# The first projection in eight units of 256 tokens, its LayerNorm on two engines and its weight casts on three, and two value products moved between the key and query products

## The chip, the cores and the metric

The kernel runs on one core of a Trainium2 chip. The metric is the device time in microseconds (us) of the whole program. Five engines work side by side and each runs its own list of instructions strictly in order, waiting on semaphores: TensorE (PE, matmuls and transposes), VectorE (DVE), ScalarE (ACT), GpSimd (POOL) and SyncE (SP, which here only issues DMA transfers). SBUF is the on-chip memory, PSUM the accumulators that TensorE writes.

## The reference, cut to what matters

One layer over 16 learned meta tokens and 512 tokens of width 1024: a first LayerNorm, one wide projection whose columns are the queries, keys and values of a sparse branch (A), its indexer, the low-rank latents of a dense branch (B) and two gates; then attention in both branches, 8 heads each, and an output projection with a second LayerNorm.

```
h = layer_norm(concat([meta, x]), ln_emb_g, ln_emb_b)
qa, ka, va, ga, qi, ki, wi, cq, ckv, kpe, gb = split(h @ w_in)
qb = rms_norm(cq) @ w_uq;  k_nope, vb = rms_norm(ckv) @ w_ukv;  rotary on q_pe and k_pe
A: scores of the indexer -> top 128 keys of each query -> softmax over them with a relative bias -> oa
B: causal softmax over all keys -> ob
out = layer_norm(ALPHA * h + concat([oa * silu(ga), ob * silu(gb)]) @ w_out, ln_post_g, ln_post_b)
```

## The kernel before, in words

**Layout.** The normalised input is held transposed, features on the partitions: `hh` and `hl`, 8 chunks of 128 features by 528 tokens. A float32 value is carried as a high part (rounded to the matmul's type, `hh`) and a low part (what the rounding left, `hl`); weights likewise as `wh` and `wl`. Each product is three matmuls: high by high, high by low, low by high. Weights come in blocks of 128 columns (`BLOCKS`), by DMA into one of three `raw` buffers, are cast to `wh` by ACT (`high_part`, L576) and subtracted into `wl` by POOL (`low_part`, L569).

**One list for all engines.** `schedule()` writes one list, `ORDER`, of stages: ("W", b) prepares weight block b, ("J", kind, n, m) is one product of the projections (a "job"), ("S", g) the scores of head g, ("X", g) its exponentials, ("R", g) its division, ("TP", g) and the job "tq" its transposes, ("PV", pair, part) the product with the values, ("TOPK", round, half) one round of the search for the top keys. Every engine walks the same list and takes its own part of each stage, in this order. Heads g = 0 to 7 are the dense branch, two heads to a pair, and 8 to 15 the sparse one. During the dense heads, DVE also does the 14 rounds of the search (MAX8 and MATCH_REPLACE8), between its other work.

**The first job.** Ahead of the list stands the opening. DVE takes the statistics of the meta tile and the four token tiles (L961, L962, L969), ACT the square root and the normalisation in place (L755, L760). TensorE passes the time with dummy transposes (`busy`, L1280). When all five tiles are normalised, it transposes chunk by chunk (`spread(c)`, L1302, four 128x128 transposes into the PSUM bank `hbank(c)`); DVE and ACT in turns apply gain and bias on the bank (L994, L767), ACT rounds it to `hh` (L772), DVE subtracts to `hl` (L999). TensorE multiplies each chunk by the first two weight blocks, which make the latent query "cq": two matmuls of 512 columns each at L1382, L1387 and L1391, and the last chunk at L1399. DVE casts these two weight blocks (L989), POOL makes their low parts in two instructions (L664), and the next product is "ckv" (L1319).

**Places the change touches later.** "qn" and "kn" are the dense branch's per-pair queries and keys: q of pair p+1 is put between the scores and the exponentials of head g = 2p+1, its two k products after the division. They are emptied from PSUM by ACT and DVE, one half each (L823, L1066; L827, L1070). "va" are the value rows of the sparse branch, four row blocks of 128 and a short one, twice; ACT alone empties them (L836). A job writes one of two PSUM banks in turn and waits until that bank's previous job has been emptied; the scores of the next pair wait until its q and both k are emptied.

Of the kernel before, what the change touches and what calls it, by code (L numbers as in the profile page):

```python
# [25 lines left out]
P = 128  # L26
# [70 lines left out]
HIGH_BY_DVE = [b in (("cq", 0), ("cq", 1)) for b in BLOCKS]  # L97
# [17 lines left out]
def schedule():  # L115
# [84 lines left out]
    for g in range(2 * HEADS):  # L200
# [124 lines left out]
def build(nc, x, meta, ln_emb_g, ln_emb_b, rel_bias, ln_post_g, ln_post_b, weights, gains, onehot, cos_t,  # L325
# [6 lines left out]
    with ctx:  # L332
# [107 lines left out]
        w_high_dve = sem("w_high_dve")  # L440
        scaled = sem("scaled")
# [103 lines left out]
        def low_made(eng, b):  # L545

            eng.wait_ge(w_low, max(LOW_BY_DVE[:b + 1].count(False), 2))
# [10 lines left out]
        def high_made(eng, b):  # L558

            if HIGH_BY_DVE[b]:  # L560
                eng.wait_ge(w_high_dve, HIGH_BY_DVE[:b + 1].count(True))
            else:
                eng.wait_ge(w_high, HIGH_BY_DVE[:b + 1].count(False))

# [39 lines left out]
        def _(sp):  # L604
            sp.dma_start(x_meta, meta).then_inc(x_in[4], 16)
            for t in range(QT):
# [31 lines left out]
        def _(pool):  # L638
# [15 lines left out]
            for i in range(QT):  # L654
                last = mask[:, POFF[i] + NK[i] - 144:POFF[i] + NK[i]]
                pool.affine_select(out=last, in_=last, compare_op=ALU.is_ge, fill=MASKED, base=META,
                                   pattern=[[-1, 144]], channel_multiplier=1).then_inc(made, 1)
            for stage, *arg in ORDER:
                if stage == "W":
                    if arg[0] == 0:  # L660
                        pool.wait_ge(w_high_dve, 2)
                        for n in range(0, DC, DC // 2):
                            c = slice(n, n + DC // 2)
                            pool.tensor_tensor(wl[:, c, 0:2 * P].rearrange("p c (b n) -> p b c n", b=2), raw[:, 0:2, c, :],  # L664
                                               wh[:, c, 0:2 * P].rearrange("p c (b n) -> p b c n", b=2).bitcast(F32),
                                               ALU.subtract).then_inc(w_low, 1)
# [989 lines left out]
```

## Time and profile before

| | us |
|---|---|
| median of 3 runs | 334.42 |
| lowest, highest run | 333.64, 335.16 |
| the profiled execution, its own time | 335.0 |
| its span, first to last instruction | 333.2 |

The profiled execution is 0.6 us slower than the median, and 1.8 us of its time lie outside the span. Its mean granted TensorE clock is 0.991 of full speed. "Busy" is the time in which an engine has an instruction running; in a timeline, the bracket at the end of a row is how long the engine sat idle before it, and what it was released by. Matmuls overlap, so a row's duration is longer than the step from one start to the next.

### The profile page before, as it was taken

To read this page: it belongs to the slowest core of one execution; us is meant where nothing else is said; L and a number is where in the kernel's file an instruction comes from. 1 tells how busy PE (TensorE), PEld (TensorE's weight loads), DVE (VectorE), ACT (ScalarE), POOL (GpSimd) and SP (SyncE) were. 2 spreads that over 40 slices of the span, in tenths; PEclk is the share of its full clock that TensorE was granted. 3 is DMA by queue.
4 is the path that set the end of the run, shared out by engine and by line. 5 is a ranking of instruction groups with operands and counts; after the bars stand their busy time and mean duration, and the time that the engine had idled before them with its cause. 6 is when DMAs were issued, how large, how long until landed. Compare 5 with 4: busy or idle time off the path is not lost.

```text
span 333.2 us, 6144 instructions
## 1 busy us (share of the span) xinstructions
PE 319.4 (96%) x2098; PEld 275.9 (83%) x2098; DVE 235.9 (71%) x626; ACT 174.6 (52%) x382; POOL 199.2 (60%) x240
## 2 busy tenths in 40 slices
PE   8799999999999999989999999999999999999990
PEld 7588987778787888878797988897978898998990
DVE  5784720259965699999995995478787866564686
ACT  4685754343543355467545664677587753722220
POOL 6260899988432251556633589699859582660552
PEclk9799999999999999999999999999999999999998
DMA  7455432428513033202400232222323110130033
GB/s 270 190 147 223 131 94 95 128 74 296 176 63 127 1 107 100 79 0 73 136 2 16 65 129 97 91 77 92 98 92 95 66 35 30 66 126 2 2 122 130
DMA packets 11710, 32.86 MB, mean 99 GB/s; under 512 B 2409, under 2 KB 2793, under 8 KB 11681
## 3 DMA queue, kind: packets, MB, share of 16 engines
q1 hardware_dynamic: 8944, 26.89, 23.7%
q10 hardware_dynamic: 2736, 5.59, 5.5%
q8 instruction: 17, 0.28, 0.3%
q14 instruction: 13, 0.10, 0.1%
HBM read 29.83 MB, written 4.81 MB: 104 GB/s over the span
## 4 chain that ended last, share of the span: by engine, by line
PE 82%; DVE 10%; issue 2%; DMA 2%; ACT 2%; SPq 1%; DVEq 0%
PE ps_j L1319 50%; PE ps_o L1579 6%; PE ps_s L1530 4%; PE ps_s L1534 3%; DVE iw L1146 3%; PE ps_t L1319 3%; PE ps_s L1503 2%; DVE top L1142 2%; PE ps_t L1549 2%; DMA iw<-in_onehot 2%; PE ps_j L1371 2%; PE ps_t L1554 2%; ACT pr L910 1%; PE ps_j L1419 1%; PE ps_j L1382 1%
## 5 line engine op out<-in xcount | busy, mean ns | idle before, releaser
L569 POOL TENSOR_TENSOR wl<-raw,wh 128x1024 fp32r<-128x1024 f32 (+2 forms) x33 | 78.1, 2374 | 56.9 <-ACT wh L576 56.8
L1319 PE MATMUL ps_j<-hh,wh 128*128 128x512 f32 (+2 forms) x216 | 75.2, 348 | 0.1
L1319 PE MATMUL ps_j<-hl,wh 128*128 128x512 f32 (+2 forms) x216 | 74.7, 346 | 0.0
L1319 PE MATMUL ps_j<-hh,wl 128*128 128x512 f32 (+2 forms) x216 | 74.4, 345 | 0.0
L705 POOL TENSOR_SCALAR pr<-pr,rden 128x528 f32<-128x528 f32 (+1 forms) x64 | 35.3, 572 | 42.5 <-DVE rden L1186 42.5
L1319 PEld LDWEIGHTS ps_j<-hh,wh 128*128 128x128 f32 (+1 forms) x216 | 40.3, 186 | 6.3 <-issue 0.5
L1319 PEld LDWEIGHTS ps_j<-hh,wl 128*128 128x128 f32 (+1 forms) x216 | 40.3, 187 | 5.1
L1319 PEld LDWEIGHTS ps_j<-hl,wh 128*128 128x128 f32 (+1 forms) x216 | 40.3, 186 | 5.1
L910 ACT ACTIVATE pr<-pr,mn 128x528 f32<-128x528 f32 (+1 forms) x64 | 36.0, 564 | 14.4 <-DVE mn L1175 14.3
L576 ACT ACTIVATE wh<-raw 128x1024 fp32r<-128x1024 f32 (+2 forms) x35 | 35.9, 1040 | 0.4 <-DMA raw<-in_weights 0.4
L723 POOL TENSOR_TENSOR bm<-bias,mask 128x144 f32<-128x144 f32 (+3 forms) x32 | 27.5, 895 | 0.0
L1146 DVE MATCH_REPLACE8 iw<-top,iw 128x512 f32<-128x512 f32 (+2 forms) x42 | 22.6, 542 | 0.0
L1142 DVE MAX8 top<-iw 128x8 f32<-128x512 f32 (+2 forms) x42 | 21.8, 547 | 0.1
L814 ACT ACTIVATE mix<-ps_j 128x512 f32<-128x512 f32 x7 | 4.2, 599 | 30.2 <-PE ps_j L1319 30.2
L1530 PE MATMUL ps_s<-k_b,q_b 96*128 96x240 f32 (+4 forms) x80 | 19.5, 390 | 0.0
L1076 DVE TENSOR_TENSOR ks<-ps_j,ks 64x264 fp32r<-64x264 f32 x32 | 13.8, 430 | 7.0 <-ACT ks L848 6.2
L1319 PE MATMUL ps_j<-wh,mbh 128*128 128x256 f32 x64 | 18.4, 287 | 0.0
L1319 PE MATMUL ps_j<-wl,mbh 128*128 128x256 f32 x64 | 18.1, 283 | 0.0
L1319 PE MATMUL ps_j<-wh,mbl 128*128 128x256 f32 x64 | 18.1, 283 | 0.0
L848 ACT ACTIVATE ks<-ps_j 64x264 fp32r<-64x264 f32 x32 | 12.3, 386 | 9.3 <-PE ps_j L1319 8.6
L1319 PE MATMUL ps_j<-wh,hh 128*128 128x256 f32 x56 | 17.0, 304 | 0.0
L920 ACT ACTIVATE pt<-ps_t 128x512 f32<-128x512 f32 x16 | 9.6, 598 | 13.6 <-PE ps_t L1549 7.7
(292 smaller groups left out, 832.8 us busy)
## 6 DMA issues: line engine op xcount, KB each, us to landing
raw<-in_weights SPq DMA_DIRECT2D x37, 512.0 KB, 3.3
bias_by_distance<-bias_vector ACTq DMA_DIRECT2D x1, 2624.0 KB, 12.7
bias<-bias_by_distance ACTq DMA_DIRECT2D x8, 264.0 KB, 2.9
res<-in_x SPq DMA_DIRECT2D x4, 512.0 KB, 5.2
out<-res SPq DMA_DIRECT2D x3, 512.0 KB, 2.6
pt<-in_ln_emb_g SPq DMA_DIRECT2D x1, 512.0 KB, 5.5
pt<-in_ln_emb_b SPq DMA_DIRECT2D x1, 512.0 KB, 6.5
q_b<-qpe ACTq DMA_DIRECT2D x8, 64.0 KB, 2.0
```

The lines of the kernel that those rows point to most:

```text
L569: eng.tensor_tensor(ring_of(False, b), raw_of(b), ring_of(True, b).bitcast(F32), ALU.subtract).then_inc(done, 1)
L576: act.activation(ring_of(True, b), raw_of(b), ACT.Copy).then_inc(w_high, 1)
L705: pool.tensor_scalar(a, a, rden[:, k, n:n + 1], 1.0, ALU.mult, ALU.mult).then_inc(scaled, 1)
L723: pool.tensor_tensor(bm[:, h % 2, s], bias[:, h % 4, T - NK[i]:T], mask[:, s], ALU.add).then_inc(folded, 1)
L848: act.activation(ks[HD * v:HD * v + HD, e, v, 264 * m:264 * m + 264], bank[HD * e:HD * e + HD, 0:264], ACT.Copy).then_inc(job_act, 1)
L910: act.activation(dst, dst, ACT.Exp, bias=mn[:, k, n:n + 1], scale=-1.0, accum_out=den[:, k, n:n + 1]).then_inc(e_done, 1)
L1076: dve.tensor_tensor(ks[HD - HD * v:P - HD * v, e, v, s], bank[HD * e:HD * e + HD, 0:264], ks[HD * v:HD * v + HD, e, v, s].bitcast(F32), AL ...
L1142: dve.max(top8[:, i, :], a).then_inc(done, 1)
L1146: dve.match_replace(out=a, in_to_replace=top8[:, i, :], in_values=a, imm_value=TAKEN).then_inc(done, 1)
L1319: last = pe.matmul(dst, a, b, start=n == 0 and part[0], stop=n == count - 1 and part[1])
L1530: last = pe.matmul(dst, q_b[:, e, i * P:(i + 1) * P], k_b[:, e, a:b], start=True, stop=True)
L1579: last = pe.matmul(ps_o[HD * e:HD * e + HD, q0:NQ], v[:, j, c:c + HD], pt[:, e, CO[j]:CO[j] + NQ - q0], start=j == 0, stop=j == 4)
```

## The change

**Opening.** The first job is cut into 8 units: unit u is two feature chunks (2i, 2i+1, with i = u mod 4) by 256 tokens (the first half for u < 4). The first half needs only token tiles 0 and 1, so TensorE can begin with those. Normalisation: ACT does the meta tile and tile 0 as before; tiles 1, 2 and 3 are done by DVE, each in two `tensor_scalar` instructions of 512 columns on SBUF. Gain and bias are two instructions of 256 columns each per unit, on DVE for units 1, 5, 7 and on ACT for the others. The first two weight blocks arrive in halves between the token tiles; the first halves are cast by ACT and DVE, the second halves and the whole of block 2 by POOL, which also makes the low parts in four steps in place of two. The six dummy transposes ahead of each of two waits go, and the first 36 become 30. The four DVE instructions on the meta columns now come after the last unit's low part. The last unit's low products are ordered by bank: two matmuls finish the first cq product, two the second; before, six finished each.

**List.** At g = 1 (pair 0) the job va(0, 2) moves from behind the division to a place ahead of qn(1), between the scores and the exponentials. At g = 5 (pair 2) the job va(1, 2) moves from ahead of kn(3, 0) to between kn(3, 0) and kn(3, 1).

The diff, cut to what matters (shifted counts of semaphores, and the statistics that are only rewritten as functions, are left out):

```diff
-HIGH_BY_DVE = [b in (("cq", 0), ("cq", 1)) for b in BLOCKS]
+FIRST_BLOCKS = 2
+GAIN_BY_DVE = [u in (1, 5, 7) for u in range(DC)]
...
-            if g % 2 and more:
-                jobs = [("qn", p + 1)] + jobs + [("kn", p + 1, 0), ("kn", p + 1, 1)]
+            if g == 1:
+                jobs += [("qn", p + 1), ("kn", p + 1, 0), ("kn", p + 1, 1)]
+            elif g % 2 and more:
+                jobs = [("qn", p + 1), ("kn", p + 1, 0)] + jobs + [("kn", p + 1, 1)]
...
-        if jobs[0][0] == "qn":
-            order.append(("QPE", jobs[0][1]))
-            job(*jobs.pop(0), extra=0)
+        if ("qn", p + 1) in jobs:
+            order.append(("QPE", p + 1))
+            while jobs[0][0] != "kn":
+                job(*jobs.pop(0), extra=0)
...
+        def unit(u):
+            i, a = u % 4, u // 4
+            return (2 * i, 2 * i + 1), slice(META + 256 * a, META + 256 * a + 256)
...
+            tile_in(0)
+            tile_in(1)
             sp.dma_start(gain[:, :], gains).then_inc(par_in, 16)
             sp.dma_start(rb[:, :], rel_bias).then_inc(par_in, 16)
             sp.dma_start(oh_sb, onehot).then_inc(oh_in, 16)
-            for b in range(len(BLOCKS)):
+            tile_in(2)
+            for half in range(2):
+                c = slice(4 * half, 4 * half + 4)
+                for b in range(FIRST_BLOCKS):
+                    sp.dma_start(raw[:, b, c, :], weights[b, :, c, :]).then_inc(raw_in[b] if half else first_in[b], 16)
+                if half == 0:
+                    tile_in(3)
...
+            def first_low(n):
+                c = slice(2 * n, 2 * n + 2)
+                pool.tensor_tensor(wl[:, c, 0:2 * P].rearrange("p c (b n) -> p b c n", b=2), raw[:, 0:2, c, :],
+                                   wh[:, c, 0:2 * P].rearrange("p c (b n) -> p b c n", b=2).bitcast(F32),
+                                   ALU.subtract).then_inc(w_low, 1)
+            pool.wait_ge(w_first_act, 1)
+            pool.wait_ge(w_high_dve, 1)
+            first_low(0)
+            first_low(1)
+            for b in range(FIRST_BLOCKS):
+                pool.wait_ge(raw_in[b], 16)
+                pool.tensor_copy(wh[:, 4:8, b * P:b * P + P], raw[:, b, 4:8, :]).then_inc(w_high_pool, 1)
+            pool.wait_ge(w_high_pool, 2)
+            first_low(2)
+            first_low(3)
+            pool.wait_ge(raw_in[2], 16)
+            pool.tensor_copy(ring_of(True, 2), raw_of(2)).then_inc(w_high_pool, 1)
...
+            def gains_of(u):
+                act.wait_ge(x_t, u + 2)
+                for n, c in enumerate(unit(u)[0]):
+                    half = hbank(u)[:, 256 * n:256 * n + 256]
+                    act.activation(half, half, ACT.Identity, bias=bcol[:, c:c + 1],
+                                   scale=gcol[:, c:c + 1]).then_inc(h_aff_act, 1)
+            def high(u):
+                chunks, s = unit(u)
...
+                act.activation(hh[:, chunks[0]:chunks[1] + 1, s], hbank(u).rearrange("p (c n) -> p c n", c=2),
+                               ACT.Copy).then_inc(h_high, 1)
+            deviation(0)
+            normal(0, 2)
+            deviation(1)
+            normal(1, 4)
+            deviation(2)
...
+            act.activation(wh[:, 0:4, 0:P], raw[:, 0, 0:4, :], ACT.Copy).then_inc(w_first_act, 1)
             act.wait_ge(par_in, 32)
...
+            gains_of(0)
+            high(0)
+            high(1)
+            deviation(3)
+            gains_of(2)
+            high(2)
+            gains_of(3)
+            deviation(4)
+            high(3)
+            gains_of(4)
+            high(4)
+            high(5)
+            gains_of(6)
+            high(6)
+            high(7)
...
+            def inverse(n, done):
+                t, r = TILES[n]
+                dve.wait_ge(root, n + 1)
+                dve.reciprocal(rstd[0:r, t:t + 1], rstd[0:r, t:t + 1]).then_inc(shift, 1)
+                dve.wait_ge(shift, done)
+                if n < 2:
+                    dve.scalar_tensor_tensor(out=nmr[0:r, t:t + 1], in0=mv[0:r, t, 0:1], scalar=-1.0,
+                                             in1=rstd[0:r, t:t + 1], op0=ALU.mult, op1=ALU.mult).then_inc(shift, 1)
+                else:
+                    for x in (0, 512):
+                        part = res[:, t, x:x + 512]
+                        dve.tensor_scalar(part, part, mv[:, t, 0:1], rstd[:, t:t + 1], ALU.subtract,
+                                          ALU.mult).then_inc(xn_dve, 1)
...
+            def low(u):
+                chunks, s = unit(u)
+                dve.wait_ge(h_high, u + 1)
+                c = slice(chunks[0], chunks[1] + 1)
+                dve.tensor_tensor(hl[:, c, s], hbank(u).rearrange("p (c n) -> p c n", c=2), hh[:, c, s].bitcast(F32),
+                                  ALU.subtract).then_inc(h_low, 1)
+            stat(0, 0)
+            stat(0, 1)
+            stat(1, 0)
+            inverse(0, 1)
+            stat(1, 1)
+            stat(2, 0)
+            inverse(1, 3)
+            stat(2, 1)
+            stat(3, 0)
+            inverse(2, 5)
+            dve.wait_ge(first_in[1], 16)
+            dve.tensor_copy(wh[:, 0:4, P:2 * P], raw[:, 1, 0:4, :]).then_inc(w_high_dve, 1)
+            dve.wait_ge(par_in, 32)
+            gains_of(1)
+            stat(3, 1)
+            low(0)
+            low(1)
+            stat(4, 0)
+            stat(4, 1)
+            inverse(3, 6)
+            low(2)
+            inverse(4, 7)
+            low(3)
+            gains_of(5)
+            low(4)
+            gains_of(7)
+            low(5)
+            low(6)
+            low(7)
...
-            busy(36)
-            pe.wait_ge(xn_done, 1)
...
+            def high(u):
+                chunks, s = unit(u)
+                a = 256 * (u // 4)
+                if u % 4 < 2:
+                    pe.wait_ge(w_first_act, 1)
+                    pe.wait_ge(w_high_dve, 1)
+                else:
+                    pe.wait_ge(w_high_pool, 2)
+                pe.wait_ge(h_high, u + 1)
+                for c in chunks:
+                    for k in range(2):
+                        pe.matmul(ps_j[:, k, a:a + 256], wh[:, c, k * P:k * P + P], hh[:, c, s], start=c == 0, stop=False,
+                                  skip_group_check=True)
+                pe.wait_ge(w_low, u % 4 + 1)
+                for c in chunks:
+                    for k in range(2):
+                        pe.matmul(ps_j[:, k, a:a + 256], wl[:, c, k * P:k * P + P], hh[:, c, s], start=False, stop=False,
+                                  skip_group_check=True)
+            def low(u):
+                chunks, s = unit(u)
+                a = 256 * (u // 4)
+                pe.wait_ge(h_low, u + 1)
+                for k in range(2):
+                    for c in chunks:
+                        last = pe.matmul(ps_j[:, k, a:a + 256], wh[:, c, k * P:k * P + P], hl[:, c, s], start=False,
+                                         stop=c == DC - 1, skip_group_check=True)
+                    if u == DC - 1:
+                        last.then_inc(job_mm, 1)
...
+            pe.wait_ge(xn_act, 2)
+            pe.wait_ge(xn_dve, 1)
+            spread(0)
+            spread(1)
+            pe.wait_ge(xn_dve, 2)
+            spread(2)
+            spread(3)
+            high(0)
+            high(1)
+            low(0)
+            low(1)
+            high(2)
+            high(3)
+            low(2)
+            pe.wait_ge(xn_dve, 6)
+            spread(4)
+            spread(5)
+            low(3)
+            spread(6)
+            high(4)
+            spread(7)
+            low(4)
+            high(5)
+            low(5)
+            high(6)
+            low(6)
+            high(7)
+            low(7)
```

**How instructions stand.** On DVE in the opening, before (the end of the statistics, then the meta columns, the weight casts and the chunks):

```order
L966 RECIPROCAL rstd<-rstd 128x1
L972 SCALAR_TENSOR_TENSOR nmr<-mv,rstd 128x1
L979 TENSOR_TENSOR iw<-ps_t,gain 128x128
L981 TENSOR_TENSOR iw<-iw,gain 128x128
L983 CAST hh<-iw 128x8x16
L985 TENSOR_TENSOR hl<-iw,hh 128x8x16
L989 CAST wh<-raw 128x8x128 x2
L994 TENSOR_SCALAR ps_s<-ps_s,gain 128x512
L999 TENSOR_TENSOR hl<-ps_s,hh 128x512
L994 TENSOR_SCALAR ps_t<-ps_t,gain 128x512
L999 TENSOR_TENSOR hl<-ps_o,hh 128x512
L999 TENSOR_TENSOR hl<-ps_t,hh 128x512
```

On DVE now, from the second half of tile 2's statistics to unit 3's low part (`res<-res,mv,rstd` is the normalisation of a token tile):

```order
L1032 BN_STATS st<-res 128x6
L1035 BN_AGGR mv<-st 128x2
L1065 TENSOR_TENSOR hl<-ps_s,hh 128x2x256
L1065 TENSOR_TENSOR hl<-ps_o,hh 128x2x256
L1032 BN_STATS st<-res 128x6 x2
L1035 BN_AGGR mv<-st 128x2
L1041 RECIPROCAL rstd<-rstd 128x1
L1049 TENSOR_SCALAR res<-res,mv,rstd 128x512 x2
L1065 TENSOR_TENSOR hl<-ps_t,hh 128x2x256
L1041 RECIPROCAL rstd<-rstd 128x1
L1049 TENSOR_SCALAR res<-res,mv,rstd 128x512 x2
L1065 TENSOR_TENSOR hl<-ps_s,hh 128x2x256
```

What moved: two token tiles are normalised between the low parts of units 1 and 3, and the meta columns are gone from here. On POOL at the same place before (ahead of the first `wl` row it makes masks), the low parts of blocks 0 and 1, then of 2 and 3:

```order
L652 AFFINE_SELECT ci<-ci 128x128
L656 AFFINE_SELECT mask<-mask 128x144 x4
L664 TENSOR_TENSOR wl<-raw,wh 128x2x4x128 x2
L569 TENSOR_TENSOR wl<-raw,wh 128x8x128
L569 TENSOR_TENSOR wl<-raw,wh 128x8x104
```

and now:

```order
L681 AFFINE_SELECT mask<-mask 128x144 x4
L687 TENSOR_TENSOR wl<-raw,wh 128x2x2x128 x2
L697 CAST wh<-raw 128x4x128 x2
L687 TENSOR_TENSOR wl<-raw,wh 128x2x2x128 x2
L702 CAST wh<-raw 128x8x128
L583 TENSOR_TENSOR wl<-raw,wh 128x8x128
L583 TENSOR_TENSOR wl<-raw,wh 128x8x104
```

What moved: three casts have come to POOL between the low parts. On ACT around the exponentials of head 1, before (`v_a` is va, `q_b` and `k_b` are qn and kn, L910 the exponentials):

```order
L836 ACTIVATE v_a<-ps_j 128x256
L857 DMA q_b<-qpe 32x512 x2
L823 ACTIVATE q_b<-ps_j 64x512
L910 ACTIVATE pr,den<-pr,mn 128x528
L910 ACTIVATE pr,den<-pr,mn 128x272
L910 ACTIVATE pr,den<-pr,mn 128x144
L910 ACTIVATE pr,den<-pr,mn 128x400
L836 ACTIVATE v_a<-ps_j 128x256
L827 ACTIVATE k_b<-ps_j 64x264 x2
L920 ACTIVATE pt<-ps_t 128x512
```

and now:

```order
L905 ACTIVATE v_a<-ps_j 128x256
L926 DMA q_b<-qpe 32x512 x2
L905 ACTIVATE v_a<-ps_j 128x256
L892 ACTIVATE q_b<-ps_j 64x512
L980 ACTIVATE pr,den<-pr,mn 128x528
L980 ACTIVATE pr,den<-pr,mn 128x272
L980 ACTIVATE pr,den<-pr,mn 128x144
L980 ACTIVATE pr,den<-pr,mn 128x400
L896 ACTIVATE k_b<-ps_j 64x264 x2
L990 ACTIVATE pt<-ps_t 128x512
```

What moved: the emptying of va(0, 2) stands ahead of that of qn(1), and so ahead of the exponentials; TensorE's matmuls stand likewise.

In pair 2 one of the two `k_b` copies of ACT goes ahead of the `v_a` one in the same way.

## Rows read from the trace of the kernel before

**Rows 1.** The page's first part: busy time, share of the span, instructions.

```profile
PE 319.4 (96%) x2098; PEld 275.9 (83%) x2098; DVE 235.9 (71%) x626; ACT 174.6 (52%) x382; POOL 199.2 (60%) x240
```

**Rows 2.** Timeline, TensorE, opening: start, duration (us), engine, line, operation, idle before.

```profile
10.64 1.02 PE L1296 MATMUL ps_s<-iw,rb 32*8 32x512 f32 x2 [2.19 <-DMA iw<-in_onehot]
...
14.14 1.11 PE L1302 MATMUL ps_s<-ident,res 128*128 128x128 f32 x4
...
18.42 0.60 PE L1302 MATMUL ps_s<-ident,res 128*128 128x128 f32 x4
...
30.18 0.36 PE L1319 MATMUL ps_j<-hh,wh 128*128 128x264 f32 x1
```

**Rows 3.** Windows by stretch: busy per engine (instructions), granted TensorE clock, DMA share, GB/s.

```profile
13.00:14.00 1.00, 1.00 (x6) 0.93 (x5) 0.97 (x4) 1.00 (x1) 0.00 (x0) 0.50 0.03 12
```

**Rows 4.** Timelines, TensorE, ACT and DVE, around the exponentials of head 1.

```profile
144.46 0.37 PE L1319 MATMUL ps_j<-ckh,wh 128*128 128x264 f32 x1 [0.92 <-ACT v_a L836]
...
141.60 0.74 ACT L910 ACTIVATE pr<-pr,mn 128x528 f32<-128x528 f32 x1 [0.79 <-DVE mn L1175]
...
143.85 0.36 ACT L836 ACTIVATE v_a<-ps_j 128x256 f32<-128x256 f32 x1
...
142.09 0.69 DVE L1066 TENSOR_SCALAR q_b<-ps_j 64x512 f32<-64x512 f32 x1
```

**Rows 5.** Timeline, TensorE, kn(3, 1) of pair 2.

```profile
181.77 0.36 PE L1319 MATMUL ps_j<-ckh,wh 128*128 128x264 f32 x1 [0.31 <-ACT v_a L836]
```

**Rows 6.** Timeline, ACT, opening: meta normalised, gain and bias, rounding, emptying of cq.

```profile
6.47 1.23 ACT L760 ACTIVATE pt<-pt,nmr,rstd 16x1024 f32<-16x1024 f32 x1
...
16.71 0.75 ACT L767 ACTIVATE ps_o<-ps_o,gain 128x512 f32<-128x512 f32 x1
17.48 0.60 ACT L772 ACTIVATE hh<-ps_o 128x512 fp32r<-128x512 f32 x1
...
29.44 0.60 ACT L786 ACTIVATE v_b<-ps_j 128x512 f32<-128x512 f32 x1 [3.49 <-PE ps_j L1399]
```

**Rows 7.** Timeline, DVE, opening: weight casts, gain and bias on PSUM.

```profile
13.26 1.29 DVE L989 CAST wh<-raw 128x1024 fp32r<-128x1024 f32 x2
15.30 0.82 DVE L994 TENSOR_SCALAR ps_s<-ps_s,gain 128x512 f32<-128x512 f32 x1 [0.75 <-PE ps_s L1302]
```

**Rows 8.** Groups by form, POOL: busy us, mean ns, idle before.

```profile
L569 POOL TENSOR_TENSOR wl<-raw,wh 128x512 fp32r<-128x512 f32 x1 | 1.3, 1302 | 0.1
...
L690 POOL COPY k_b<-k_b 32x528 f32<-32x528 f32 x1 | 0.6, 622 | 0.1
```

**Rows 9.** Timelines, POOL and DVE, 75 to 81 us: both on SBUF.

```profile
75.86 2.39 POOL L569 TENSOR_TENSOR wl<-raw,wh 128x1024 fp32r<-128x1024 f32 x1 [0.80 <-ACT wh L576]
78.33 1.66 POOL L685 TENSOR_TENSOR k_b<-k_b,cos_sb 32x528 f32<-32x528 f32 x1
...
75.96 2.84 DVE L1102 SCALAR_TENSOR_TENSOR v_b<-v_b,gain,pr 128x512 f32<-128x512 f32 x1
...
75.96 4.57 DVE L1102 SCALAR_TENSOR_TENSOR v_b<-v_b,gain,pr 128x512 f32<-128x512 f32 x2
```

**Rows 10.** Timelines, DVE and POOL, at 198 us: `tensor_scalar` on SBUF beside POOL.

```profile
197.69 0.55 DVE L1152 TENSOR_SCALAR mask<-drop 128x128 bf16<-128x128 f32 x1
195.73 2.42 POOL L569 TENSOR_TENSOR wl<-raw,wh 128x1024 fp32r<-128x1024 f32 x1
...
198.16 0.29 DVE L1152 TENSOR_SCALAR mask<-iw 128x256 bf16<-128x256 f32 x1
...
198.11 0.84 POOL L705 TENSOR_SCALAR pr<-pr,rden 128x528 f32<-128x528 f32 x1
```

**Rows 11.** The chain that ended last: start, duration, what (va's 24 matmuls, later).

```profile
148.54 2.84 PE ps_j L1319 x24
```

**Rows 12.** Timelines, DVE and TensorE, ahead of head 4's scores.

```profile
161.70 0.79 DVE L1070 COPY k_b<-ps_j 64x264 f32<-64x264 f32 x2
...
162.63 1.08 PE L1530 MATMUL ps_s<-k_b,q_b 96*128 96x240 f32 x4
```

More of the change, by code:

```diff
@@ L440, in build @@
         w_high_dve = sem("w_high_dve")
+        w_high_pool = sem("w_high_pool")
+        w_first_act = sem("w_first_act")
+        xn_dve = sem("xn_dve")
+        xn_act = sem("xn_act")
+        first_in = [sem(f"first_in{b}") for b in range(FIRST_BLOCKS)]
         scaled = sem("scaled")
@@ L748, in spread_bias @@
                 act.dma_start(bias[:, h % 4, :], src).then_inc(bias_in[h], 16)
-            for n in range(6):
-                if n < 5:
-                    t, r = TILES[n]
-                    act.wait_ge(stats, n + 1)
-                    act.activation(rstd[0:r, t:t + 1], mv[0:r, t, 1:2], ACT.Sqrt, bias=eps_ln[0:r, 0:1]).then_inc(root, 1)
-                if n:
-                    t, r = TILES[n - 1]
-                    src = x_meta if t == 4 else res[:, t, :]
-                    act.wait_ge(shift, 2 * n)
-                    act.activation(src[0:r, :], src[0:r, :], ACT.Identity, bias=nmr[0:r, t:t + 1],
-                                   scale=rstd[0:r, t:t + 1]).then_inc(xn_done, 1)
@@ L763, in _, with deviation @@
[L763 to L774 removed]
+            def deviation(n):
+                t, r = TILES[n]
+                act.wait_ge(stats, n + 1)
+                act.activation(rstd[0:r, t:t + 1], mv[0:r, t, 1:2], ACT.Sqrt, bias=eps_ln[0:r, 0:1]).then_inc(root, 1)
@@ new lines, in normal @@
+            def normal(n, need):
+                t, r = TILES[n]
+                src = x_meta if t == 4 else res[:, t, :]
+                act.wait_ge(shift, need)
+                act.activation(src, src, ACT.Identity, bias=nmr[0:r, t:t + 1],
+                               scale=rstd[0:r, t:t + 1]).then_inc(xn_act, 1)
+            def gains_of(u):
[4 more added lines that the diff above has]
+                                   scale=gcol[:, c:c + 1]).then_inc(h_aff_act, 1)
@@ L953, in _, with stat @@
             dve.wait_ge(eps, 2)
[L956 to L959 removed]
+            def stat(n, half):
+                t, r = TILES[n]
+                src = x_meta if t == 4 else res[:, t, :]
+                if half == 0:
                     dve.wait_ge(x_in[t], 16)
[L961 to L967 removed]
+                dve.bn_stats(st[0:r, t, half, :], src[0:r, 512 * half:512 * half + 512]).then_inc(bn_s, 1)
+                if half == 1:
@@ new lines, in gains_of @@
+            def gains_of(u):
+                dve.wait_ge(x_t, u + 2)
+                for n, c in enumerate(unit(u)[0]):
+                    half = hbank(u)[:, 256 * n:256 * n + 256]
+                    dve.tensor_scalar(half, half, gcol[:, c:c + 1], bcol[:, c:c + 1], ALU.mult,
+                                      ALU.add).then_inc(h_aff, 1)
+            def low(u):
[4 more added lines that the diff above has]
+                                  ALU.subtract).then_inc(h_low, 1)
@@ L1282, in _ @@
             pe.wait_ge(made, 2)
[L1283 to L1284 removed]
+            busy(30)
+            pe.wait_ge(xn_act, 1)
             for c in range(DC):
@@ new lines, in low @@
+            def low(u):
+                chunks, s = unit(u)
+                a = 256 * (u // 4)
+                pe.wait_ge(h_low, u + 1)
+                for k in range(2):
+                    for c in chunks:
[3 more added lines that the diff above has]
+                        last.then_inc(job_mm, 1)
```

120 lines of the change are left out of this document (26 added, 94 removed).

## The prediction

> **What bounds the kernel now.** I read the page's busy shares first, then the timelines of the opening, then the waits of TensorE. TensorE is busy 96% of the span, no other engine over 71% [rows 1], so time is won or lost only where TensorE stands idle, runs at half clock, or is made to wait anew. In the opening it transposes the first tile at 14.14 and starts ckv at 30.18 [rows 2]. Between these two it has 48 matmuls of 512 columns and 32 transposes and no wait that shows. The granted clock was 0.50 from 13 to 14 us [rows 3], which is the 1.2 GHz level, after TensorE had stood idle 2.19 us until 10.64; four transposes took 1.11 us at that level and 0.60 at the other [rows 2]. What the opening costs is therefore the 14.14 us before the first transpose. Later TensorE waits 0.92 us in pair 0 [rows 4] and some 0.45 us in pair 2 [rows 5], each time before the second k product, since ACT empties va behind the exponentials or behind va's own end.
>
> **The opening, step by step.** All times here are estimates, worked from rows.
>
> Start. ACT normalises the meta tile in 1.23 us from 6.47 [rows 6]. Now it is first and can start at about 5.7, when its own reciprocal is there; it ends at 6.9. A square root and DVE's answer, 0.6, then tile 0 in 1.23, to 8.7; another square root 0.3; then DVE normalises the first half of tile 1 and TensorE can start at about 9.7. That is 4.4 us earlier than 14.14. If nothing else were late, most of it would be won.
>
> DVE. A half tile by `tensor_scalar` on SBUF has no row. The nearest are the cast on SBUF, 1024 columns in 0.65 [rows 7], so about 0.4 for 512, and gain and bias on PSUM, 0.82 for 512 [rows 7]. I take 0.5, nearest the SBUF row. Then DVE does: tile 1 to 10.0; half a weight cast, 0.4; wait for unit 1's transposes until 11.6; two gains of 256 columns, 0.9; statistics, 0.8; two low parts, to 14.7; tile 3's statistics, 1.4. So at 16.2 it asks for tile 2's first half. Gain and bias on ACT keep pace: 0.75 for 512 columns [rows 6], and 256 columns fewer take 0.24 less (0.60 against 0.36 in [rows 4, 6]), so 0.5 each.
>
> POOL. Low parts in four steps: 1.30 for 512 columns [rows 8], I take 1.2; a cast of 512 columns 0.6 by the copy of 528 in 0.622 [rows 8]. From 10.5, when both first casts are there: 1.2, 1.2, 0.6, 0.6, 1.2, 1.2, to 16.6. Then come the cast of block 2, 1.1, and its low part, 2.4.
>
> The two together. When DVE and POOL both work on SBUF they take turns. DVE's instruction of 75.96 took 2.84 while POOL had one until 78.25; POOL's next, started at 78.33, went through, and DVE's second ended only at 80.53 [rows 9]. `tensor_scalar` is held in the same way: a 128-column one took 0.55 and ended just behind POOL's 2.42 [rows 10]. So in the changed opening: DVE 16.6 to 17.1, POOL's cast to 18.1, DVE's second half to 18.6, unit 2's low part (on PSUM, beside POOL) to 19.2, then tile 3's halves wait for POOL's low part of block 2 until 20.8 and end at 21.7. Without turns they would end at 18.8.
>
> TensorE. It has run out of work by then (about 3.3 us idle in two waits) and begins the second half's transposes at 21.8. Behind them lie four groups of transposes at 0.44, one low product at 0.47 and four units at 12 x 0.118 = 1.41 (24 matmuls of 256 columns took 2.84 [rows 11]), 7.9 in all, and about 0.9 of waits for ACT's rounding of unit 4 and DVE's low part of unit 5: end at 30.6. One thing more is late: ckv needs the bank of the first cq product, which ACT empties in 0.60. Before, that stood ready 0.9 us ahead of the end (from 29.44 [rows 6]); now its last matmul is only 0.24 ahead, so the emptying shows with about 0.6. Ckv starts at 31.3 against 30.18: **1.1 us later**. The shorter dummy transposes, the earlier loads and the later meta columns (four instructions of 0.3, hidden behind the last four low products) cost nothing here; if TensorE did not lag, the meta columns would show with 0.8. From 30.18 to 124 us TensorE does not wait in the trace of before, and what feeds it is released by its own products, so the shift goes through whole.
>
> By the Trainium skill (SBUF — State Buffer, "Who interferes with whom") DVE and GpSimd hold a shared port pair for a whole instruction, and whoever starts first gets it. The turns of [rows 9] agree. But DVE's 256-column instruction of 198.16 took only 0.29 although POOL's had started at 198.11 [rows 10]; by the rule it would have waited. By the rule the sum is the 31.3 above; by that row it is the first rival.
>
> **Pair 0.** Before, qn(1) was emptied at 140.21, and ACT began the exponentials at 141.60, when DVE gave the minima [rows 4]. Now va(0, 2), 2.84 us [rows 11], comes first: qn ends about 142.9, ACT empties it and starts the exponentials at 143.55, 1.95 later. DVE stands idle too, from 142.09 [rows 4] to 143.0, since its emptying of qn(1) is queued ahead of the search, and again before the divisions; it takes up the search 1.3 us later than before. The wait of 0.92 goes, but the k products are now emptied behind the later exponentials, and the next scores wait for them: 0.7 us later there. At head 4's scores TensorE started at 162.63, right behind DVE's k copies of 161.70 [rows 12]; DVE's lag arrives there with 1.2. So **+1.2 us**. Bounds: -0.92, if the wait goes and nothing comes; +1.3, DVE's whole lag.
>
> **Pair 2.** DVE and ACT are both idle there; the k copy is done while va runs, and the 0.45 of [rows 5] goes: **-0.45**. The bank of "tq" is then va's, emptied while the transposes run.
>
> **Sum.** 1.1 + 1.2 - 0.45 = +1.85 on a span of 333.2 with 1.8 outside it: 336.85 for a run like the profiled one of 335.0, and 336.2 against the median of 334.42, which lies 0.6 under that run.
>
> **Rivals.**
>
> *DVE gets through between POOL's instructions.* If DVE's second half follows its first as at 198.16, or block 2's weights come late enough that POOL has nothing queued, the two tiles end at about 19.3 and ckv starts 2.3 earlier than forecast, at about 29.0, 1.2 us before 30.18; with no turns at all it would be 28.4, 1.8 before. With the middle between its own bounds (-1.4 for both waits gone, +0.75 as above) that is 331.2 to 334.0, centre 332.6: on the faster side. For it: the first transposes really can start 4.4 us earlier, and [rows 10]. Against: [rows 9]. It decides at the point where POOL's low part of block 2 starts before or after tile 3's first half.
>
> *`tensor_scalar` with its scalars read per partition isn't held and takes 0.8 as on PSUM.* Then no turns: the tiles end at 20.3, ckv starts at about 29.8, -0.4; with the middle's +0.75: 334.8.
>
> *Half clock.* TensorE idles 3.3 us between 18 and 21.8; a wait of 2.19 us was followed by the clock of 0.50 [rows 2, 3]. If it falls after these waits for as long as it did there, a part of the second half's 7.9 us of products runs at half speed, less what the waits in between take up: 1.1 more, 337.3.
>
> *The middle works as its waits suggest.* DVE's lag has slack that I don't see, both waits go (-1.4), the opening is as forecast: 334.1.
>
> **How the numbers follow.** Forecast 0.41 (335.2 to 337.0: half over 336.1), DVE through 0.27, `tensor_scalar` free 0.12, half clock 0.12, middle works 0.08. A measurement of this kernel can tell about 0.5%, 1.7 us, from no change. Faster (under 332.7): 0.18 from the first rival, 0.02 from the tails. Slower (over 336.1): 0.26 of the forecast, 0.12 of the clock, 0.01: 0.39. Within: 0.41. The range leaves out the lower third of the first rival (0.11) and the upper half of the clock's (0.07): 332.0 to 337.4.
>
> **What would show it.** Right: in the profile after, the first transposes near 9.7; DVE's four instructions that normalise tiles 2 and 3 with some well over 1 us, each ending just behind a POOL one; a TensorE wait of 2 us near 20; ckv at 31; DVE's search after head 1's exponentials 1.3 us later relative to ckv; head 6's scores 0.75 later. Wrong: those four all near 0.5, or no wait of TensorE over 1 us in the opening. If ckv starts before 29.5, the first rival holds; if TensorE's wait in pair 0 is gone and head 4's scores are not later relative to ckv, my middle is wrong.

## The result, and the profile after

The changed kernel takes 338.01 us (median of 6 runs, 337.20 to 340.34) against 334.61 of the kernel before in the same rounds. The ratio is 1.0114, with a 95% interval of 1.0077 to 1.0151, so 2.6 to 5.1 us slower. I had forecast slower, but 336.2, and the time lies outside my range (332.0 to 337.4).

The profiled execution took 339.22 us, with a span of 337.3 and 1.9 outside it; the span is 4.1 over that of before. The page's first line reads as in [rows 1]:

```profile
PE 321.1 (95%) x2128; PEld 280.1 (83%) x2128; DVE 240.6 (71%) x630; ACT 172.5 (51%) x385; POOL 201.5 (60%) x245
```

TensorE's timeline in the opening answers to [rows 2] (start, duration, engine, line, operation; in brackets the idle time before it and its releaser):

```profile
9.86 0.64 PE L1409 MATMUL ps_s<-ident,res 128*128 128x128 f32 x4 [0.43 <-DVE res L1049]
...
19.24 0.74 PE L1439 MATMUL ps_j<-hl,wh 128*128 128x256 f32 x4 [1.08 <-DVE hl L1065]
21.59 1.11 PE L1409 MATMUL ps_s<-ident,res 128*128 128x128 f32 x4 [1.61 <-DVE res L1049]
...
32.32 0.63 PE L1439 MATMUL ps_j<-hl,wh 128*128 128x256 f32 x4
33.49 0.36 PE L1484 MATMUL ps_j<-hh,wh 128*128 128x264 f32 x1 [0.55 <-ACT v_b L855]
```

It transposes the first tile 4.3 us earlier, waits 2.7 us in two waits for DVE, and starts ckv 3.3 us later than before. The timelines of DVE and POOL show why DVE is late, as [rows 9] did for another place:

```profile
9.17 1.00 DVE L1049 TENSOR_SCALAR res<-res,mv,rstd 128x512 f32<-128x512 f32 x2
...
15.96 2.63 DVE L1049 TENSOR_SCALAR res<-res,mv,rstd 128x512 f32<-128x512 f32 x2
...
19.29 2.24 DVE L1049 TENSOR_SCALAR res<-res,mv,rstd 128x512 f32<-128x512 f32 x2
...
14.59 2.54 POOL L687 TENSOR_TENSOR wl<-raw,wh 128x512 fp32r<-128x512 f32 x2
17.07 1.23 POOL L702 CAST wh<-raw 128x1024 fp32r<-128x1024 f32 x1
18.39 2.41 POOL L583 TENSOR_TENSOR wl<-raw,wh 128x1024 fp32r<-128x1024 f32 x1
```

For tile 1 (at 9.17), with POOL idle, the two instructions took 1.00 together; for tiles 2 and 3 they take 2.63 and 2.24, and the pairs end 0.3 and 0.7 us behind a POOL instruction (at 18.59 behind 17.07 + 1.23, at 21.53 behind 18.39 + 2.41). The windows by stretch (columns as in [rows 3]; the granted clock is the third number from the end) show what follows TensorE's waits (the first row is for tile 2's pair and is used below):

```profile
16.00:17.00 1.00, 1.00 (x11) 1.00 (x10) 1.00 (x1) 0.72 (x3) 1.00 (x1) 1.00 0.00 0
20.00:21.00 1.00, 0.00 (x0) 0.00 (x0) 1.00 (x1) 0.00 (x0) 0.80 (x1) 0.79 1.20 302
21.00:22.00 1.00, 0.41 (x2) 0.41 (x3) 1.00 (x3) 0.00 (x0) 0.00 (x0) 0.50 1.21 258
24.00:25.00 1.00, 1.00 (x7) 1.00 (x6) 1.00 (x3) 0.73 (x2) 0.00 (x0) 0.50 1.06 414
27.00:28.00 1.00, 1.00 (x9) 1.00 (x8) 0.28 (x1) 0.00 (x0) 0.00 (x0) 0.80 0.62 239
```

The clock falls to 0.50, the 1.2 GHz level, within the wait (20.6) and stays there until 27.4, so nearly all transposes of the second half and the products of unit 4 run at half speed. A first stretch of 0.50 lies at 10.3 to 13.8, where before had one from 12.9 to 16.3; it makes DVE's gain of unit 1 start 0.4 later (11.47, against 11.03 in a profile without that stretch), which disappears behind DVE's waits for POOL.

In the middle TensorE's waits, of which before had two of 0.92 and 0.31 [rows 4, 5], now read (engine, line, releaser: total, times, longest):

```profile
PE ps_j L1536 <- DVE k_b L1177: 1.5, 2, 1.2
...
PE ps_j L1484 <- DVE q_b L1173: 0.5, 1, 0.5
```

Measured from the start of ckv, the scores behind pair 0 come 0.81 later than before, those of head 4 1.22 later, and those of head 6, behind pair 2, 0.67 later. The sum of the profile is 3.31 (ckv) + 1.22 (pair 0) - 0.55 (pair 2) + 0.1 behind head 6 = 4.1.

### The profile page after: what moved, and what is told of

Read it like the earlier page. It is cut to its first block, busy times and chain, and to the rows that moved or that the text cites. A ratio compares the mean times of both kernels' runs of the same rounds, so it can differ in the third digit from the quotient of the medians.

```text
span 337.3 us, 6229 instructions
## 1 busy us (share of the span) xinstructions
PE 321.1 (95%) x2128; PEld 280.1 (83%) x2128; DVE 240.6 (71%) x630; ACT 172.5 (51%) x385; POOL 201.5 (60%) x245
## 4 chain that ended last, share of the span: by engine, by line
PE 83%; DVE 11%; ACT 2%; issue 2%; DMA 1%; DVEq 0%; ACTq 0%
PE ps_j L1484 53%; PE ps_t L1484 6%; PE ps_o L1719 5%; PE ps_s L1670 4%; PE ps_s L1674 3%; PE ps_s L1643 2%; PE ps_t L1689 2%; DVE res L1049 2%; PE ps_j L1536 1%; ACT pr L980 1%; PE ps_t L1694 1%; DVE st L1032 1%; DVE top L1249 1%; DVE iw L1253 1%; PE ps_s L1409 1%
## 5 line engine op out<-in xcount | busy, mean ns | idle before, releaser
L590 ACT ACTIVATE wh<-raw 128x1024 fp32r<-128x1024 f32 (+2 forms) x34 | 34.9, 1040 | 0.6 <-DMA raw<-in_weights 0.6
L761 POOL TENSOR_TENSOR bm<-bias,mask 128x144 f32<-128x144 f32 (+3 forms) x32 | 27.4, 891 | 0.0
L1249 DVE MAX8 top<-iw 128x8 f32<-128x512 f32 (+2 forms) x42 | 21.8, 547 | 0.1
L883 ACT ACTIVATE mix<-ps_j 128x512 f32<-128x512 f32 x7 | 4.2, 598 | 30.2 <-PE ps_j L1484 30.2
L1670 PE MATMUL ps_s<-k_b,q_b 96*128 96x240 f32 (+4 forms) x80 | 19.5, 390 | 0.0
L1183 DVE TENSOR_TENSOR ks<-ps_j,ks 64x264 fp32r<-64x264 f32 x32 | 13.8, 430 | 7.0 <-ACT ks L917 6.2
```

Source lines behind the costliest of these rows:

```text
L590: act.activation(ring_of(True, b), raw_of(b), ACT.Copy).then_inc(w_high, 1)
L761: pool.tensor_tensor(bm[:, h % 2, s], bias[:, h % 4, T - NK[i]:T], mask[:, s], ALU.add).then_inc(folded, 1)
L1183: dve.tensor_tensor(ks[HD - HD * v:P - HD * v, e, v, s], bank[HD * e:HD * e + HD, 0:264], ks[HD * v:HD * v + HD, e, v, s].bitcast(F32), AL ...
L1249: dve.max(top8[:, i, :], a).then_inc(done, 1)
L1670: last = pe.matmul(dst, q_b[:, e, i * P:(i + 1) * P], k_b[:, e, a:b], start=True, stop=True)
```

## The experiments

Ratios are to the kernel before on the same chip, in the same rounds. "ckv" is the start of the ckv job, 30.18 in the profile before.

**The opening alone, and the list alone.** The first undoes the list's edits in the changed kernel (its diff is the one shown, cut), the second makes them in the kernel before:

```diff
-            if g == 1:
-                jobs += [("qn", p + 1), ("kn", p + 1, 0), ("kn", p + 1, 1)]
-            elif g % 2 and more:
-                jobs = [("qn", p + 1), ("kn", p + 1, 0)] + jobs + [("kn", p + 1, 1)]
+            if g % 2 and more:
+                jobs = [("qn", p + 1)] + jobs + [("kn", p + 1, 0), ("kn", p + 1, 1)]
```

> The change without its edits of the list: pair 0 and pair 2 are as in the kernel before. Theory, from the two traces: the opening made ckv 3.3 us later (33.49 against 30.18), the list added 0.8 (4.1 at head 6's scores): so this kernel is about 0.8 faster than the changed one, near 337.2, and ckv starts between 31.3 and 33.5 by how long the granted clock stays at 0.50. Rival: the list's new waits of TensorE (0.51, 1.20 and 0.27) count in full, 2.0, less the 1.2 that it removes elsewhere only in part: this kernel at 336.0.

> The kernel before with the list edits alone (va(0, 2) ahead of qn(1) in pair 0, va(1, 2) between the k products in pair 2), the opening as before. Theory: +1.2 by head 4's scores, -0.5 at head 6's, so +0.75 in all, 335.4; ckv unmoved at 30.2. Rival: in the changed kernel DVE's lag there came partly from the opening (work left over from it), and alone the list gives +0.2 or less, 334.8.

The opening alone: 337.49 where 337.2 was expected, ratio 1.0082 (1.0052 to 1.0113). The list alone: 335.83, ratio 1.0022 (0.9997 to 1.0047), which is 0.7 us where 0.75 was expected. The two products make 1.0104, near the 1.0114 of both. The list is a small part of the loss; the opening is the rest. In the profile of the list alone, ACT's exponentials of head 1 start at 145.18, 7.20 behind the scores of 137.98; before, these numbers were 141.60 and 136.34, so 5.26. That is 1.94 more, where I had worked out 1.95. One expectation failed: ckv started at 31.82 in this profile and not at 30.2. The list has no part in that, since its edits come later; the clock has, as shown further down.

The opening alone had ckv at 31.95. TensorE's longest wait and the clock around it:

```profile
21.46 1.12 PE L1406 MATMUL ps_s<-ident,res 128*128 128x128 f32 x4 [2.40 <-DVE res L1046]
...
20.00:21.00 1.00, 0.00 (x0) 0.00 (x0) 1.00 (x1) 0.00 (x0) 1.00 (x1) 0.92 1.18 270
22.00:23.00 1.00, 1.00 (x6) 1.00 (x5) 0.00 (x1) 0.39 (x1) 0.00 (x0) 0.50 1.01 197
24.00:25.00 1.00, 1.00 (x10) 1.00 (x9) 1.00 (x3) 0.73 (x2) 0.00 (x0) 0.87 1.03 373
```

Here the stretch of 0.50 lasted 3.4 us; in the profile of the changed kernel it was 6.8.

**POOL out of DVE's way.** One wait, ahead of the cast of block 2:

```diff
             pool.wait_ge(raw_in[2], 16)
+            pool.wait_ge(xn_dve, 6)
             pool.tensor_copy(ring_of(True, 2), raw_of(2)).then_inc(w_high_pool, 1)
```

> The changed kernel, but POOL waits with the cast of block 2 and its low part until DVE has normalised tile 3. Theory (turns at SBUF, then the clock): tile 3's two halves take about 1.1 instead of 2.24 and are done near 19.4, the second half's transposes begin near 19.5 instead of 21.59, TensorE's waits shrink from 2.7 to about 1; ckv 2.1 earlier if the clock falls as before (time about 336), and about 4.5 earlier if it doesn't fall then (about 333.6). Rival: DVE's normalisation is long because of the DMAs that write SBUF at that time (the share is 1.07 to 1.21 from 19 to 22 us), not because of POOL: tile 3's halves still take 2.2 and the time stays at 338.

335.52, ratio 1.0016 (0.9998 to 1.0034). DVE's two pairs, and TensorE's second half, in its profile:

```profile
15.53 2.24 DVE L1050 TENSOR_SCALAR res<-res,mv,rstd 128x512 f32<-128x512 f32 x2
...
18.48 1.00 DVE L1050 TENSOR_SCALAR res<-res,mv,rstd 128x512 f32<-128x512 f32 x2
...
19.53 0.66 PE L1410 MATMUL ps_s<-ident,res 128*128 128x128 f32 x4 [0.37 <-DVE res L1050]
```

Tile 2, which still has POOL's low parts beside it, takes 2.24 (2.63 in the changed kernel). Tile 3, which has no POOL instruction beside it, takes 1.00. This run alone doesn't exclude the DMAs, since holding POOL back also held back the next weights: DMA had a share of 0.28 during tile 3's pair here, and 1.17 in the changed kernel. The trace of the changed kernel does: tile 2's pair took 2.63 with a DMA share of 0.00 (the window from 16 to 17 us above), and tile 1's took 1.00 with 0.97. So the length is POOL's doing and not that of the DMAs or of the instruction, and the rival falls. The granted clock was 1.00 from 8 to 320 us. Ckv started at 29.39, near the 29.0 (4.5 earlier) expected for a clock that stays up; the time expected with it, 333.6, was too low by 1.9, in part because it takes 4.5, a difference of the profiled execution of the changed kernel, off the median, and that execution was 1.2 slower than the median, with the longest stretch of 0.50. One wait on the engine that had time to spare bought back nearly all of the opening's loss.

**TensorE kept busy in its waits.** The changed kernel with dummy transposes into unused PSUM columns; all else, DVE's lateness too, stays:

```diff
+            def fill(count):
+                for _ in range(count):
+                    pe.transpose(ps_t[:, 384:512], ident[:, :], ident[:, :])
...
             high(3)
+            fill(8)
             low(2)
+            fill(13)
             pe.wait_ge(xn_dve, 6)
```

> The changed kernel with 8 dummy transposes ahead of unit 2's last products and 13 ahead of the wait for tile 3, on unused columns of PSUM, so that TensorE hardly stands idle from 17.9 to 21.6. Theory (the idle time brings the clock of 0.50 that lasted from 20.8 to 27.2): the granted clock stays at 1.00 after 14, the second half still begins at 21.6, and ckv starts near 31.0, 2.5 earlier than in the changed kernel's profile; the time falls to about 335.5. Rival: the clock falls for another reason (the whole opening's load), then the half-clock stretch stays and with it 338.

337.05, ratio 1.0068 (1.0040 to 1.0095). In its profile:

```profile
21.35 0.65 PE L1409 MATMUL ps_s<-ident,res 128*128 128x128 f32 x4 [0.20 <-DVE res L1049]
...
31.21 0.36 PE L1490 MATMUL ps_j<-hh,wh 128*128 128x264 f32 x1 [0.55 <-ACT v_b L855]
...
21.00:22.00 1.00, 0.80 (x8) 0.66 (x7) 0.89 (x2) 0.00 (x0) 0.00 (x0) 1.00 0.71 139
24.00:25.00 1.00, 1.00 (x10) 1.00 (x10) 0.39 (x1) 1.00 (x3) 0.00 (x0) 1.00 1.00 393
```

The second half begins as late as in the changed kernel, the clock stays up, and ckv starts at 31.21. It is this kernel, the change without its half clock, that my sum described: 31.3 for ckv, +1.85 in all; it showed 31.21 and +0.68%, 2.3, and in the second run below 31.69 and +0.93%, 3.1. The time of 335.5 that I expected of it was too low: I had taken the 2.5 us off one profile, in which the stretch of 0.50 was the longest that I saw.

Both were run again on one chip, side by side:

> The changed kernel once more, to stand on one chip beside the filled one. Both theories: ratio about 1.011 to the kernel before, mean granted clock 0.976 to 0.989 in most executions.

> The changed kernel with 21 dummy transposes in TensorE's two waits, once more. Theory (the half clock behind the two waits is what my sum left out): 1.2 to 1.5 faster than the changed kernel beside it, ratio to the kernel before 1.0055 to 1.007, and mean clocks of 0.99 and more. Rival (the difference between the earlier two came from the chips): both at the same ratio within 0.002.

The changed kernel: 338.78, ratio 1.0114 (1.0085 to 1.0143), mean clocks 0.985 to 0.993. With dummies: 337.73, ratio 1.0093 (1.0072 to 1.0113), mean clocks 0.994 and 0.995. The difference of 1.05 us has the expected sign, but it is less than the 1.2 to 1.5 expected, the ratio lies above the expected 1.0055 to 1.007, the ratios' difference of 0.0021 is at the edge of what the rival allowed, and the intervals overlap; timing alone would not settle it. The clocks and the profiles do. Of the eighteen timed executions of the changed opening as it is (changed kernel, again, opening alone), seventeen had a mean clock of 0.990 or less; the one with 0.993 took 336.94, the fastest of its six. Of the thirteen with dummies, twelve had 0.991 or more. A mean says that the clock fell, not where. The profiles say where: from the start of the second half to ckv it took 9.86 us in both profiles with dummies, and 11.90, 10.93 and 10.49 in the three of the changed opening as it is (changed kernel, again, opening alone), whose stretches of 0.50 lasted 6.8, 3.4 and 3.4 (ckv at 33.49, 32.28 and 31.95). So the half clock cost 2.0, 1.1 and 0.6 in these three.

**The reverse: the kernel before, kept busy.** One line, in TensorE's wait of 2.19 [rows 2]:

```diff
+            busy(16)
             pe.wait_ge(oh_in, 16)
             pe.wait_ge(par_in, 32)
```

> The kernel before with 16 dummy transposes in TensorE's wait of 2.19 us ahead of the vector product of the opening, nothing else. Theory (standing idle is what brings the clock of 0.50 that follows, 12.94 to 16.34 in its profile): the granted clock stays at 1.00 through the opening, the first four chunks' transposes and the first products run at full speed, ckv starts near 29.1 instead of 30.18, and the time falls by about 1. Rival: the clock falls at the start of real work whatever was done before; then the stretch of 0.50 stays, and the time with it.

334.33, ratio 0.9964 (0.9944 to 0.9984), in 12 runs that lie within 0.8 us of one another. The clock at the place of [rows 3], ACT's normalisation of the last two tiles, the first transposes, and ckv:

```profile
13.00:14.00 1.00, 1.00 (x11) 0.95 (x10) 0.84 (x2) 0.39 (x1) 0.07 (x1) 1.00 0.00 0
...
11.03 2.36 ACT L760 ACTIVATE res<-res,nmr,rstd 128x1024 f32<-128x1024 f32 x2
...
13.46 0.63 PE L1303 MATMUL ps_s<-ident,res 128*128 128x128 f32 x4
...
29.17 0.36 PE L1320 MATMUL ps_j<-hh,wh 128*128 128x264 f32 x1
```

Time and clock came as expected, and ckv 1.0 earlier. But the clock is not the whole of that 1.0. In the profile before, ACT's same row reads

```profile
11.73 2.36 ACT L760 ACTIVATE res<-res,nmr,rstd 128x1024 f32<-128x1024 f32 x2
```

so ACT was done at 14.09, and the first transposes of 14.14 [rows 2] could hardly have come earlier at any clock; with the dummies ACT was done at 13.39. From the first transposes to ckv it took 16.04 before and 15.71 here: 0.3 is the clock's in this pair of profiles. Three more profiles of this opening bear it out. With dummies and ACT done at 14.30 (the first run under "Together"), ckv started at 30.05 at full clock. Without dummies, but with a wait of only 1.25 in place of 2.19 (the next run), the clock stayed at 1.00 and ckv started at 29.07. And in the list alone, a wait of 1.70 came with a clock of 0.50 from 10.5 to 17.3:

```profile
15.83 1.06 PE L1305 MATMUL ps_s<-ident,res 128*128 128x128 f32 x4
...
31.82 0.36 PE L1322 MATMUL ps_j<-hh,wh 128*128 128x264 f32 x1
```

There the dummies and small products at half speed held the first transposes until 15.83, 1.66 behind ACT's 14.17, and the clock cost 1.9 in all. So the half clock of the kernel before cost nothing, 0.3 or 1.9, by whether it fell and for how long, and what 16 instructions that compute nothing win in the median, 1.2 us here, depends on how often it falls. On this chip 20 of the 35 executions of the kernel before had a mean clock of 0.986 or less (median 335.38); on the chip of the two repeated runs and of those under "Together" it was 4 of 20 (median 334.35).

**Another list.** Since pair 2's edit works, the same order in pair 0 (qn, then kn, va, kn, all but qn behind the exponentials), in the kernel before:

```diff
             if g % 2 and more:
-                jobs = [("qn", p + 1)] + jobs + [("kn", p + 1, 0), ("kn", p + 1, 1)]
+                jobs = [("qn", p + 1), ("kn", p + 1, 0)] + jobs + [("kn", p + 1, 1)]
```

> The kernel before with another list: in pair 0 too the value product stands between the two k products, as the change has it in pair 2, and qn(1) stays where it was, ahead of the exponentials. Theory (what cost time in pair 0 was that va went ahead of qn, so that the exponentials and DVE's search began later): both waits go, 0.92 and 0.45 to 0.55, and nothing comes in their place: 1.4 less, ratio about 0.996. Rival: DVE's search is late at head 4 whatever the order of TensorE, since its k copies now come at another place: the gain of pair 0 is given back there, -0.5 in all.

336.79, ratio 1.0050 (1.0026 to 1.0075), where 0.996 was expected: wrong, by sign. TensorE, DVE and the clock in pair 0:

```profile
141.83 0.36 PE L1319 MATMUL ps_j<-wh,hh 128*128 128x256 f32 x1 [2.39 <-DVE q_b L1066]
...
140.99 0.69 DVE L1066 TENSOR_SCALAR q_b<-ps_j 64x512 f32<-64x512 f32 x1
...
143.00:144.00 1.00, 1.00 (x7) 1.00 (x7) 0.53 (x4) 0.11 (x1) 0.75 (x2) 0.50 0.00 0
```

va now takes the PSUM bank of qn, and DVE's emptying of qn stands behind its minima, which it began at 139.17, when the search let it. TensorE had only the three matmuls of the k product in between, to 139.4. The old order had va in the other bank there, 2.8 us of work. In pair 2 the products with the values of pair 1 stand between qn and the k product (20 matmuls, 2.53 us), so qn is emptied by the time va comes; pair 0 has no pair before it, and so not this cover. And the wait of 2.39 in the middle of full work was followed by the clock of 0.50, from 142.7 to 146.1. Neither theory had this.

**Tile 3 on ACT.** ACT stood idle from 16.7 to 22.7 in the changed kernel. It now normalises tile 3; DVE makes unit 2's low part and tile 3's scalars first; POOL's block 2 waits for tile 2 (the diff is cut to DVE's and ACT's order):

```diff
-            inverse(3, 6)
             low(2)
-            inverse(4, 7)
+            inverse(4, 6)
+            inverse(3, 7)
             low(3)
...
             high(3)
+            normal(4, 0)
             gains_of(4)
```

> The changed kernel with its list, but ACT normalises tile 3 (it stood idle from 16.7 to 22.7), DVE makes unit 2's low part and the scalars for tile 3 ahead of tile 2, and POOL's work on block 2 waits for tile 2. Theory: both tiles are ready near 18.2, TensorE's waits there shrink to under 0.5, the clock stays up, ckv starts near 28.2 against 29.4 with POOL's wait alone and 33.5 in the changed kernel: about 1.1 faster than with POOL's wait alone, ratio 0.998. Rival: the chain of gain, rounding and low part of the second half's first unit binds then, and ckv stays at 29.4, ratio 1.001.

> The last kernel with the other list (value products between the k products in both pairs). Theory: the list's 0.75 goes and 1.4 comes: 2.1 faster than the last kernel, ratio 0.992 to the kernel before. Rival: the parts don't add, since DVE's search chain needs the time that the opening gave; then 0.996.

The first: 335.38, ratio 0.9982 (0.9962 to 1.0002), ckv at 28.56 (28.2 expected). The second, with the other list: 335.51, ratio 0.9995 (0.9970 to 1.0019) where 0.992 was expected. That list costs in pair 0, as above: its profile has a wait of 2.17 there, and 0.50 from 143.2 to 146.6.

**Together.**

> The kernel before with the 16 dummies in the opening's wait and the list's edit of pair 2 alone (va(1, 2) between the two k products). Theory: pair 2's edit is worth 0.5 by itself, so the ratio goes from 0.9964 (dummies alone) to 0.995. Rival: it is given back further on, ratio 0.9964.

> The changed opening with tile 3 on ACT, POOL's work on block 2 held until tile 2 is normalised and 6 dummies ahead of the first token transposes; pair 0's list as in the kernel before, pair 2's as changed. Theory: against the same opening with the changed list (0.9982) pair 0's 1.2 goes: ratio 0.9945, ckv at 28.5. Rival: the earlier start of ckv is lost in the middle, where DVE's search sets the pace of pair 0: ratio 0.997.

Dummies and pair 2's edit in the kernel before: 333.99, ratio 0.9979 (0.9962 to 0.9995). 0.995 was expected. Against the 0.9964 of the dummies alone this doesn't show a gain; the intervals overlap, and the two ratios are from different chips, on which the kernel before itself ran differently (335.38 and 334.35 above); in the trace head 6's scores stand 152.70 behind ckv, where they stood 153.24 before, so the edit's 0.54 is there. The last kernel (tile 3 on ACT, six more dummies, pair 0 as before, pair 2 as changed): 333.26, ratio 0.9953 (0.9934 to 0.9971), where 0.9945 and ckv at 28.5 were expected. It is 1.6 us faster than the kernel before by the ratio (1.1 by the medians) and 5.5 faster than the changed one on the same chip. It keeps the change's idea of an opening in halves. Its ckv and head 6's scores:

```profile
28.27 0.36 PE L1494 MATMUL ps_j<-hh,wh 128*128 128x264 f32 x1 [0.55 <-ACT v_b L859]
...
181.01 2.43 PE L1680 MATMUL ps_s<-k_b,q_b 96*128 96x240 f32 x10
```

## Why the prediction was wrong, point by point

- *Start of the opening*: first transposes at 9.7 forecast, 9.86 measured. Right, and it brought what I said, nothing.
- *DVE and POOL take turns* (the step on which the sign hung): tile 3 done at 21.7 forecast, 21.5 measured; second half's transposes at 21.8, measured 21.59; without turns 18.8 to 19.3, and 19.5 where POOL waited for tile 3 alone. Right, and shown by taking POOL away. The rival "DVE gets through" and the rival "`tensor_scalar` is free of it" fall: `tensor_scalar` on SBUF took 0.5 for a half tile and was held.
- *TensorE from there to ckv*: 9.5 forecast, 9.86 at full clock in both profiles with dummies, the emptying of the cq bank showing with 0.55 (0.6 forecast). Right at full clock.
- *The clock*: **this is the step that failed.** I had it as a rival with a chance of 0.12 and 1.1 us, and left it out of the sum, although [rows 2, 3] showed a wait of 2.19 and the 0.50 behind it, and my own sum had TensorE idle for 3.3 us. In all three profiles of the changed opening left as it was, the clock fell in or just behind those waits; in none of the six where the waits were filled or shortened (the longest left was 0.54) did it fall there. The term was 2.0, 1.1 and 0.6 in the three; the difference of the medians with and without dummies was 1.05. The rival's price of 1.1 was about right; its chance should have been near one, by the mean clocks of the eighteen executions.
- *Pair 0*: +1.2 forecast, +1.22 at head 4; *pair 2*: -0.45 forecast, -0.55. The sum of both 0.75, measured 0.79 in the trace and 0.7 in time. Right. The rival that the middle works as its waits suggest falls.
- *What is left.* The forecast's 1.85 and 1.1 for the clock make 2.95; 3.4 was measured by the medians, 3.8 by the ratio. The runs with dummies say the same from the other side: 2.3 and 3.1 over the kernel before, against 1.85, so 0.4 to 1.3 is not the clock's. 0.1 of the rest is time outside the span (1.9 against 1.8). More may come from the first scores of pair 0, which in five of nine profiles with the changed opening, and in none of the five without, waited 0.3 to 0.9 us: the load of `q_b` ahead of them landed 2.5 to 2.8 us after its issue (median of its two) in these five, and 2.0 in the others. What makes it slower I can't say: the DMAs beside it looked alike. It stays open.

My range left out the upper half of the clock's rival. With the clock in the sum the forecast would have been 337.3, which is still 0.7 short of the median.

## What to carry to other kernels

A wait of TensorE has two prices: its own length, and the half clock that may come with it. Where a change makes TensorE wait as long as a wait that already has a clock of 0.50 behind it in the trace (2.19 here; the new ones were 2.4 to 2.7 in sum), put the second price in the sum; and if the wait can't be removed, dummy transposes in it are nearly free. The price is not the same in each execution (0.6 to 2.0 here), so don't read it off one profile. And when two profiles differ in the start of a stage, ask what released it in each, before the whole difference is put down to the clock. Before giving DVE and POOL work on SBUF in the same stretch, ask which of the two can wait: one semaphore on POOL was worth 3.3 us here, by the ratios (1.0114 to 1.0016). And an order that gains in one stage can lose in its twin if another engine's queue differs there: look at what empties the bank, and what that stands behind.

## What the runs showed of the hardware

- The clock of 0.50 came behind waits of TensorE in the midst of full work, not only at the start: a wait of 2.39 at 139.4 us was followed by 0.50 from 142.7 to 146.1. The stretches in these profiles lasted 3.4 us or 6.8.
- A wait just ahead isn't the whole condition. In the opening of the kernel before, a wait of 2.19 was followed by 3.4 us of 0.50, one of 1.70 in another execution came with 6.8 us of it, and one of 1.25 in a third with none. The changed kernel's first stretch (10.3 to 13.8) came behind an idle time of only 0.43, with dummies and small products before it, and other executions with 0.85 or 1.05 there had none. Executions of one kernel also differ: those of the kernel before had mean clocks from 0.981 to 0.994 on one chip, and with the 16 dummies 0.992 to 0.995, with times that spread 0.8 us in place of 3.2.
- By the Trainium skill (SBUF — State Buffer, "Who interferes with whom") `tensor_scalar` is one of the DVE instructions that can contend with GpSimd, and whoever issues first holds the shared port pair for the whole instruction. The runs agree for 512-column `tensor_scalar` with scalars per partition: 1.86 to 3.06 for a pair that began with POOL at work on SBUF, 1.00 without.
